# A transformer kernel in fp32: the second block's first RMS norm moves its per-token factor behind the block's linear layers

## The reference, cut to what matters

```python
def rms_norm(x, g):
    xf = xf * lax.rsqrt(jnp.mean(xf * xf, axis=-1, keepdims=True) + EPS)
    return xf * g
...
h = rms_norm(x, norm1_pre[i])
proj = h @ w_in[i]
q, k, v, z, xbc, dt_raw, gates = split_cols(proj, IN_SPLITS)
```

## Time and profile before

| what | value |
|---|---|
| median of 3 runs | 2415.89 us (2411.99 to 2418.12) |
| profiled execution, its own time | 2418.24 us |
| its span in the profile | 2416.4 us |
| TensorE busy | 93% of the span, 10848 matmuls |
| DVE, ACT, POOL busy | 47%, 41%, 40% |
| mean TensorE clock granted | 0.949 of full |

### The profile page before, as it was taken

The page is one execution under the profiler, slowest core; times in us unless marked ns, Lnnn a source line. Parts: engine busy times, 40 slices in busy tenths (PEclk is TensorE's granted clock), DMA queues, the critical chain, the costliest instruction groups (busy, mean ns, idle before and its releaser), DMA issues.

```text
span 2416.4 us, 28105 instructions
## 1 busy us (share of the span) xinstructions
PE 2252.1 (93%) x10848; PEld 1838.2 (76%) x10848; DVE 1137.8 (47%) x1828; ACT 986.4 (41%) x1995; POOL 961.9 (40%) x746
## 2 busy tenths in 40 slices
PE   7999999999979887999999888997899999999997
PEld 6787778888877776788888676664587887888886
DVE  3445565553344764655553443445644324444422
ACT  5656344443244653344442344433244334332221
POOL 3555643443456641644444341003432335222232
PEclk9999999999989998899999988877999999999998
DMA  4112122222222220132222211000002221222221
GB/s 152 53 53 71 53 91 102 99 94 99 98 74 75 79 84 18 53 105 100 92 101 96 74 52 47 20 33 18 18 29 87 95 105 70 104 88 105 92 100 53
DMA packets 29845, 183.08 MB, mean 76 GB/s; under 512 B 3984, under 2 KB 4112, under 8 KB 11920
## 3 DMA queue, kind: packets, MB, share of 16 engines
q1 hardware_dynamic: 29712, 181.27, 21.8%
HBM read 174.97 MB, written 2.10 MB: 73 GB/s over the span
## 4 chain that ended last, share of the span: by engine, by line
PE 85%; DVE 6%; ACT 4%; issue 2%; POOL 2%; DMA 1%; SPq 0%; POOLq 0%; ACTq 0%; DVEq 0%
PE PS L1319 83%; PE PS L1444 1%; PE PS L1554 1%; POOL LO L2546 1%; DVE bQS L2020 1%; DMA RAW<-wall 0%; DVE aQS L2020 0%; DVE cCVT L2430 0%; ACT HI L1642 0%; POOL A_c L2570 0%; DVE XL L2098 0%; DVE YH L2127 0%; PE PS L1492 0%; ACT bP L1860 0%; POOL bTQ L2603 0%
## 5 line engine op out<-in xcount | busy, mean ns | idle before, releaser
L2546 POOL TENSOR_TENSOR LO<-RAW,HI 128x512 fp32r<-128x512 f32 (+2 forms) x382 | 538.9, 1427 | 727.4 <-ACT HI L1642 727.4
L1319 PE MATMUL PS<-XH,HI 128*128 128x512 f32 (+1 forms) x1584 | 645.6, 408 | 30.3 <-ACT FP L1943 7.0
L1319 PE MATMUL PS<-XH,LO 128*128 128x512 f32 (+1 forms) x1584 | 628.7, 397 | 0.0
L1319 PE MATMUL PS<-XL,HI 128*128 128x512 f32 (+1 forms) x1584 | 622.8, 397 | 2.2 <-DVE XL L2098 2.1
L2020 DVE TENSOR_TENSOR LO<-RAW,HI 128x512 fp32r<-128x512 f32 (+2 forms) x286 | 304.1, 1067 | 290.0 <-ACT HI L1642 289.7
L1642 ACT ACTIVATE HI<-RAW 128x512 fp32r<-128x512 f32 (+3 forms) x668 | 365.9, 609 | 173.1 <-PE PS L1319 169.6
L1319 PEld LDWEIGHTS PS<-XH,HI 128*128 128x128 f32 (+1 forms) x1584 | 304.0, 192 | 115.1 <-issue 39.4
L1319 PEld LDWEIGHTS PS<-XH,LO 128*128 128x128 f32 (+1 forms) x1584 | 303.5, 192 | 66.9 <-issue 1.1
L1319 PEld LDWEIGHTS PS<-XL,HI 128*128 128x128 f32 (+1 forms) x1584 | 303.5, 192 | 63.0 <-DVE XL L2098 3.7
L1319 PE MATMUL PS<-HL,HI 128*128 128x512 f32 x528 | 205.4, 389 | 0.0
L1319 PE MATMUL PS<-HH,HI 128*128 128x512 f32 x528 | 205.4, 389 | 0.0
(11 more groups left out here) (382 smaller groups left out, 3372.8 us busy)
## 6 DMA issues: line engine op xcount, KB each, us to landing
RAW<-wall SPq DMA_DIRECT2D x138, 1024.0 KB, 4.8
RAW<-wall SPq DMA_DIRECT2D x24, 896.0 KB, 4.5
bROT<-bTQ SPq DMA_DIRECT2D x64, 64.0 KB, 2.0
RAW<-wall SPq DMA_DIRECT2D x5, 512.0 KB, 3.3
XF<-xT SPq DMA_DIRECT2D x4, 512.0 KB, 5.2
outT<-XR SPq DMA_DIRECT2D x8, 256.0 KB, 2.0
FP<-cfp SPq DMA_DIRECT2D x1, 1024.0 KB, 6.7
MKF<-cmask SPq DMA_DIRECT2D x1, 704.0 KB, 10.8
```

Of the source, the lines that this page charges most:

```text
L1319: return e.matmul(out, a, b, start=start, stop=stop)
L2546: return e.tensor_tensor(out, x, h.bitcast(F32), ALU.subtract)
```

## The change

- After `f1` the mean is copied from bank 5 to SBUF (`lnc`) and POOL subtracts it for blocks 2 to 7 (`lnm`), as the kernel's other layer norms do. `ln` on ACT now writes XR and, right behind it, XH = XR · gain; `xv` on DVE makes XL. The step `rms` is gone.
- The statistics of `c0` are a chore that starts after cq 0; the sums of squares are on DVE (as for `p`). They end in `rps`: ACT copies the factor along tokens to RPS, DVE keeps the per-partition form in RCT and half of it in RCH.
- cq 0, ck 0 and cq 1 take banks out of six and leave their five tiles there; `left()` evacuates them once the factor is known. Then the units go back to banks 0 and 1.
- The factor goes into outputs: `cqe` (DVE product with RPS instead of a copy, then ACT squares cQ), `cvev` (scale on ACT, and a three-operand form on DVE), `cxe` (a new POOL product of 128x512 in place on CU, which `cx1` waits for), `cze` (scales), `mga`, `mgs` (a new DVE product from PSUM into SG, then the sigmoid there).

The diff, cut to its core:

```diff
@@ -545,12 +546,6 @@
 
     def layer_norm(n, final=None):
         statistics(n, True)
-        if final is not None:
-            for j in range(8):
-                s = put("ln", n, j)
-                freed[5] = freed[6] = ("lt", s)
-                accumulate(final, j, False)
-            return
...
@@ -558,14 +553,30 @@
             if j < 8:
                 s = put("ln", n, j)
                 freed[5] = freed[6] = ("lt", s)
-            if j:
+            if j and final is None:
                 x_step[j - 1] = put("lnx", n, j - 1)
-
-    def rms_apply(n):
-        statistics(n, False)
+            elif j:
+                x_step[j - 1] = put("xv", final, j - 1)
+                ag.high_of[x_step[j - 1]] = ("ln", n, j - 1)
+
+    def deviation(n, known):
+
...
         squared, turned_q, converted = [False] * 5, [False] * 5, [False]
-        turns = []
+        turns, waiting, scaled = [], [], [False]
 
         def qk_units(key, n0, widths=(128, 128), together=False):
             for j, t in enumerate(lin_fm(key, "X", widths=widths, together=together)):
-                s = put("cqe", n0 + j, t)
-                squared[n0 + j] = True
-                freed[tiles[t].bank] = ("cqe", s)
+                waiting.append((n0 + j, t))
+            left()
+
+        def left():
+            while scaled[0] and waiting:
+                n, t = waiting.pop(0)
+                freed[tiles[t].bank] = ("cqe", put("cqe", n, t))
+                squared[n] = True
 
...
@@ -955,12 +952,16 @@
                 freed[tiles[t].bank] = ("cxe", put("cxe", 2 * i + jj, t))
                 chores.append(xconv(2 * i + jj))
 
-        lin["banks"] = [0, 1]
         put("half")
         alongside(attention(), RATES[4])
         qk_units(("cq", 0), 0, together=True)
+        chores.append(deviation("c0", scaled))
         qk_units(("ck", 0), 4, (128,))
         qk_units(("cq", 1), 2)
+        until(lambda: scaled[0])
+        left()
+        lin["banks"] = [0, 1]
+        lin["n"] = 0
 
...
                 act(blk(XR, j), NORM[n][TS[j % 3]][:, :], ACT.Identity, bias=col(GAINS[n][1], j)).then_inc(SEM["la"], 1)
+                e.wait_ge(*when("la", *step))
+                act(blk(XH, j), blk(XR, j), ACT.Copy, scale=col("n1pre", j)).then_inc(SEM["xh"], 1)
             elif kind == "lnc":
                 n, = a
...
             elif kind == "cqe":
                 n, t = a
-                e.wait_ge(*when_(ag.tiles[t].full))
-                act(SQ5[n], PS[ag.tiles[t].bank][:, :], ACT.Square).then_inc(SEM["csq"], 1)
+                e.wait_ge(*when("cqe", *step))
+                act(SQ5[n], blk(cQ, n), ACT.Square).then_inc(SEM["csq"], 1)
             elif kind == "cvev":
                 c, t = a
+                if c == 0:
+                    e.wait_ge(*when("rct", "rps", "c0"))
                 e.wait_ge(*when_(ag.tiles[t].full))
-                act(blk(cV, c, 128), PS[ag.tiles[t].bank][:, 0:128], ACT.Copy).then_inc(SEM["vev"], 1)
+                act(blk(cV, c, 128), PS[ag.tiles[t].bank][:, 0:128], ACT.Copy, scale=RCT[:, c:c + 1]).then_inc(SEM["vev"], 1)
             elif kind == "cp1":
...
             elif kind == "cx1":
                 j, = a
-                e.wait_ge(*when("cxe", *whole["cxe", j]))
+                e.wait_ge(*when("cxr", *whole["cxe", j]))
                 if j == 0:
...
+                e.wait_ge(*when("srs", "stat2", "c0", False))
+                e.tensor_copy(RCT, RSD)
+                e.tensor_scalar(RCH, RSD, 0.5, None, ALU.mult).then_inc(SEM["rct"], 1)
+            elif kind == "xv":
+                n, j = a
+                e.wait_ge(*y_made(n, j))
+                e.wait_ge(*when("xh", *ag.high_of.get(step, step)))
+                e.scalar_tensor_tensor(out=blk(XL, j), in0=blk(XR, j), scalar=col(GAINS[n], j), in1=blk(XH, j).bitcast(F32),
                                        op0=ALU.mult, op1=ALU.subtract).then_inc(SEM["xl"], 1)
             elif kind in ("n1", "fin"):
                 j, = a
...
             elif kind == "cqe":
                 n, t = a
-                e.wait_ge(*when("csq", *step))
-                e.tensor_copy(blk(cQ, n), PS[ag.tiles[t].bank][:, :]).then_inc(SEM["cqe"], 1)
+                if n == 0:
+                    e.wait_ge(*when("rps", "rps", "c0"))
+                e.wait_ge(*when_(ag.tiles[t].full))
+                e.tensor_tensor(blk(cQ, n), PS[ag.tiles[t].bank][:, :], RPS[:, :], ALU.mult).then_inc(SEM["cqe"], 1)
             elif kind == "cvev":
...
+            elif kind in ("mga", "mgs"):
+                i, j, t = a
+                x = 1024 * j + (512 if kind == "mgs" else 0)
+                e.wait_ge(*when_(ag.tiles[t].full))
+                if i > 0:
+                    e.wait_ge(*when("mxl", *whole["mps", i - 1, j]))
+                e.tensor_tensor(SG[:, x:x + 512], PS[ag.tiles[t].bank][:, :], RPS[:, :], ALU.mult).then_inc(SEM["mgr"], 1)
...
+            elif kind == "cxe":
+                j, t = a
+                e.wait_ge(*when("rps", "rps", "c0"))
+                e.wait_ge(*when("cxe", *step))
+                e.tensor_tensor(CU[j % 2], CU[j % 2], RPS[:, :], ALU.mult).then_inc(SEM["cxr"], 1)
```

More of the change, by code:

```diff
@@ L1044, in mix_a @@
             for j, t in enumerate(lin_fm(("cga", i), "X")):
-                freed[tiles[t].bank] = ("mga", put("mga", i, j, t))
+                freed[tiles[t].bank] = ("mgr", put("mga", i, j, t))
             for j, t in enumerate(lin_fm(("cpa", i), "cO")):
@@ L1050, in mix_b @@
             for j, t in enumerate(lin_fm(("cgs", i), "X")):
-                freed[tiles[t].bank] = ("mgs", put("mgs", i, j, t))
+                freed[tiles[t].bank] = ("mgr", put("mgs", i, j, t))
             for j, t in enumerate(lin_fm(("cps", i), "cY")):
@@ L1098, in agenda @@
     layer_norm("f1", final="c0")
-    rms_apply("c0")
     second()
@@ L1998, in scalar @@
                 i, j, t = a
-                e.wait_ge(*when_(ag.tiles[t].full))
-                if i > 0:
-                    e.wait_ge(*when("mxl", *whole["mps", i - 1, j]))
+                e.wait_ge(*when("mgr", *step))
                 x = 1024 * j + (512 if kind == "mgs" else 0)
-                act(SG[:, x:x + 512], PS[ag.tiles[t].bank][:, :], ACT.Sigmoid).then_inc(SEM[kind], 1)
+                act(SG[:, x:x + 512], SG[:, x:x + 512], ACT.Sigmoid).then_inc(SEM[kind], 1)
             elif kind == "mps":
```

111 lines of the change are left out of this document (45 added, 66 removed).

## The result

The changed kernel takes 2397.44 us in the median of 9 runs (2389.05 to 2404.1), the kernel before 2413.2 in 9 runs beside it (2402.99 to 2418.12): a ratio of 0.9938, with a 95% interval of 0.9918 to 0.9958. Two later comparisons of the same two kernels gave 0.9896 (0.9881 to 0.9911) and 0.9887 (0.9872 to 0.9902). So it is faster, by some 15 us in the first comparison and by 25 in the others. These runs don't settle why the two figures differ; what can move the time of one and the same kernel by some 10 us turned out to be half of the case.

A forecast was written before the change was run, and what follows sets the result against it. TensorE was taken to bound the kernel (85% of the chain that ended last), another chain the drain. Terms from +17.0 to −9.3 summed to +10.6 us: median 2415.9 to 2405.3 us, own range 2401 to 2411, outer 2397 to 2416.

The forecast's parts named there:

- rival B: Rotation hides behind cx 0 and the taps' relief in the drain stays: gain about 18, 2397.5 us; chance 0.12.
- first matmul earlier: Start of the first query unit: it reads XH as soon as ln writes it, first matmul at 1382.9, +17.0 us.
- first unit fed by blocks: First query unit, fed block by block, takes 13.25 us against 12.8 before: −0.5, up to 2 more.
- statistics in the stream: c0's statistics now stand among TensorE's matmuls, costed like the norm p: −6.0 us, −4.3 without the slow spell.
- rotation stall: cx 1 waits until all five tiles are turned; tiles 2 and 3 stand ahead of the first cxe: −9.3 us.
- wait for cADT: Softplus stands later, behind the first cx1, so TensorE's wait of 4.62 us becomes about 5.6: −1.0.
- items into the drain: Three csc, cfl and cva each move from the TensorE-bound stretch of convolutions and attention into the drain: +7.1 us.
- drain: Stretch before cb: taps run free, about 5 us less, against extra maxima, copies and later attention: 0, ±2.5 us.
- factor by POOL: Factor into outputs: cxe's 12 POOL products and the gates' DVE products cost 0.2 at a few unit ends: −1.0 us.
- A: Attention items are not saved, the drain grows by most of 7.1 us: gain 3.5, 2412.4 us; chance 0.22.
- C: POOL product between cxe and cx1 delays TensorE at each of six unit ends: slower, 2424.7 us; chance 0.06.
- D: No effect: the first unit does not start early since XH waits for something else; given no chance of its own.

The follow-up runs named there:

- e10: Changed kernel with the rate of the attention's items at 1.26 instead of 1.15, so fewer stand in the drain; 2396.98 us, ratio 0.9919 to before.
- e4: Changed kernel with the preparation steps put into the list twice as densely (SLOW 1 instead of 2); ratio 0.9927 to the kernel before.
- e7: Changed kernel with dense preparation, early evacuation, seven idle steps between cdt and cacs, and attention rate 1.05 instead of 1.15; ratio 0.9892 to before.
- e3: Changed kernel without the 12 POOL products of the token factor onto the convolution's tiles; ratio 0.9909 to the kernel before.
- e12: The changed kernel itself, unaltered, profiled a third time; median 2389.79 us, ratio 0.9887 to the kernel before.
- e8: Kernel before, with POOL's products y0 held back until the last convolution is complete (cxm 11); 2415.42 us in one run.
- e1: Changed kernel, but TensorE waits for the last block's XH before the first matmul of the first query unit; ratio 0.9975 to before.
- e2: Changed kernel with the query and key tiles put up for evacuation once the factor is known, not behind the unit; ratio 0.9899 to before.
- e11: Changed kernel with early evacuation of the query and key tiles, a second time; 2393.71 us, ratio 0.9909 to the kernel before.

## Why the prediction came out as it did

The direction, the place and nearly all terms of idle time held; the size was too small. The forecast was +10.6, to 2405.3 us; the stretch gave +14.7 in the first pair of profiles, and the medians 15.8, 24.2 and 26.1 us in the three comparisons. The first median, 2397.44, lies outside the forecast's own range of 2401 to 2411 and on the number of rival B, 2397.5, whose mechanism did not happen: that is a coincidence.

| term | forecast | measured in the first pair |
|---|---|---|
| first matmul earlier | +17.0 | 22.04 − 5.48 = +16.6 |
| first unit fed by blocks | −0.5 | 12.8 − 13.84 = −1.0, and 0.6 of waiting for LO behind it |
| banks | +2.0 | +2.0, no such wait left |
| statistics in the stream | −6.0 | 0.28 + 1.03 + 0.95 + 1.05 = −3.3 |
| rotation stall | −9.3 | 2.36 + 6.91 = −9.3 |
| wait for cxe | +2.3 | +2.3 (contained in the 6.91) |
| wait for cADT | −1.0 | 4.62 − 4.43 = +0.2 |
| items into the drain | +7.1 | about +9.5, an estimate from e10, e4 and e7, see below |
| drain | 0 | 22.25 − 24.52 = −2.3 |
| factor by POOL | −1.0 | 0 (e3: waits unchanged) |
| sum | +10.6 | +14.1 |

The 0.6 us between 14.1 and 14.7 I can't place. The signs named for a right forecast came but for two: the first XH·HI 16.6 us earlier, the idle time of 6.9 released by `cxe`, taps at 0.78; but c0's matmuls had no slow neighbours, and the wait for cADT was 4.4 us instead of 5 to 6. Some of the agreement is luck: the 2.3 us ahead of tile 3's chain were taken as "a third of a chain" without a row for it, and measured 2.36.

**Mis-sized: the items moved into the drain.** The sum had 3 × 3.18 × 0.75 = 7.1, the 0.75 for busy times that overlap. Two pairs of profiles at the same clock of 0.90 up to the end of cx 5 show what such items cost there. e10 has 3 csc, 3 cfl and 2 cva more than e12 and 8.75 us more busy time; with the 0.75 they would be 6.3, without it 8.3. e4 has 1 csc, 3 cfl and 3 cva more than e7 (1158 matmuls for 1120) and 232.56 − 226.13 = 6.4 us more; with the 0.75 they would be 5.2, without it 7.0. So the discount was too large, and 3 × 3.18 = 9.5 is the better size. It is an estimate, since the clocks of a pair agree in the mean and not from moment to moment.

**Mis-sized: the statistics.** "I take −6.0" was read from the norm `p`, with its wait of 0.95 and a slow spell of 1.7. In cq 1 neither came; the other end that the text named, −4.3 without the spell, was nearer, and without the wait it is close to the 3.3 measured.

**Right sum, wrong parts: the drain.** The text set 5 us for the taps against the extra maxima and an attention chain that ends later, and got 0 ± 2.5. It is −2.3, inside. The shape is what e8 and e10 show: `y0` beside the taps costs the drain 5.7 us in the kernel before, and with the items moved back (e10) four taps beside it take 6.74 us instead of 3.07. The changed kernel does 12 us more TensorE work in a drain that is 2.3 us longer. Both ends are needed for the move of the items to pay: the stretch ahead gives up their busy time (8.75 us in e10's pair), and the drain takes them in at hardly any length.

**Missing: a term for the clock.** The sum had the clock only where `c0`'s statistics stood. The three profiles of the changed kernel have 249.3, 249.3 and 238.8 us of busy time for the same matmuls. Together with the tail behind `cb` (741.2, 741.2 and 738.5) that is 12 us, nearly as much as the whole change in idle time. It is not chance alone. Over whole executions the mean granted clock was 0.948 to 0.953 in the 33 later runs of the kernel before, 0.950 to 0.960 in the 17 of the changed kernel, 0.951 or 0.952 in all eight of e1, and 0.957 or 0.958 in all five of e4: the kernel takes part in it. So a part of the 24 to 26 us of the later comparisons probably is clock that the change brings, beside its idle time; how much, and by what, is not shown. The forecast's own range, 5 to 15 gained, left no room for it, while the outer range down to 2397 just held the first median; the later ratios of 0.9896 and 0.9887 would lie below it. Rival B has no term for it either, and its own mechanism, a rotation that hides behind cx 0, is refuted by the wait of 6.91.

**The rivals.** A, that the moved items save nothing, falls with e10. C, POOL's product in the way of every unit's end, falls with e3, and D with the first matmul at 1376.27. The rule named with C, from the Trainium skill, "SBUF — State Buffer", section "Who interferes with whom", fits where two long operations meet: a tap beside `y0` went to 2.38 us at most, its own 0.74 and less than one product of 8.81 / 4 = 2.2 more. For the 12 products of 1.3 us it made next to nothing: without them (e3) DVE is busy 134.5 us instead of 135.4.

No version here beats the changed kernel clearly. e2, e3, e7 and e11 are level with it within the intervals of the later comparisons.
